# The V projection by seven block products for eight, over token halves, pairs of k tiles and column halves

## The reference

```python
x = x + (y * silu(gate)) @ a_w_out[layer]            # end of layer 0
kv = _rmsnorm(x, kv_norm) @ w_kv                     # (512, 2048) @ (2048, 4096)
k = kv[..., :D_ATTN].reshape(bsz, s, 16, 128)
v = kv[..., D_ATTN:].reshape(bsz, s, 16, 128)
```

## Time and profile before

| | |
|---|---|
| median of 3 runs | 1697.44 us (1697.07 to 1697.75) |
| the profiled execution, its own time | 1697.99 us |
| its span | 1696.3 us |
| PE busy | 1681.1 us (99%) |
| PE weight loads busy | 1407.6 us (83%) |
| DVE busy | 895.3 us (53%) |
| ACT busy | 778.8 us (46%) |
| POOL busy | 229.1 us (14%) |
| DMA, mean | 101 GB/s |

### The profile page before, as it was taken

The page is one execution under the profiler, slowest core; times in us unless marked ns, Lnnn a source line. Parts: engine busy times, 40 slices in busy tenths (PEclk is TensorE's granted clock), DMA queues, the critical chain, the costliest instruction groups (busy, mean ns, idle before and its releaser), DMA issues.

```text
span 1696.3 us, 23428 instructions
## 1 busy us (share of the span) xinstructions
PE 1681.1 (99%) x7839; PEld 1407.6 (83%) x7839; DVE 895.3 (53%) x1600; ACT 778.8 (46%) x1542; POOL 229.1 (14%) x219
## 2 busy tenths in 40 slices
PE   8999999999999999999999999999999999999998
PEld 6888888888888888888888888888888888888888
DVE  5666676666765343442223556464655556463333
ACT  7655566665555232333334544454444535432223
POOL 0121221112112010120000111111111111112100
PEclk9999999999999999999999999999999999999999
DMA  5333333333332222333343322223232232323223
GB/s 183 100 102 97 99 94 98 93 97 95 103 97 98 94 99 93 98 94 120 123 123 120 103 92 85 94 87 99 75 105 88 91 98 76 106 75 115 92 96 134
DMA packets 154269, 170.87 MB, mean 101 GB/s; under 512 B 9992, under 2 KB 135128, under 8 KB 154072
## 3 DMA queue, kind: packets, MB, share of 16 engines
q1 hardware_dynamic: 154200, 170.02, 31.8%
HBM read 161.59 MB, written 8.39 MB: 100 GB/s over the span
## 4 chain that ended last, share of the span: by engine, by line
PE 98%; ACT 1%; DVE 0%; DMA 0%; issue 0%; POOL 0%; SPq 0%; POOLq 0%; DVEq 0%; ACTq 0%
PE ps L398 96%; PE ps L537 1%; PE ps L427 0%; DMA xraw<-in_x 0%; PE ps L582 0%; DVE rbuf L1056 0%; POOL y_lo L1257 0%; ACT w_hi L641 0%; PE ps L434 0%; ACT abuf L729 0%; DVE w_lo L909 0%; DVE tbuf L1052 0%; ACT L729 0%; ACT rbuf L717 0%; ACT tbuf L726 0%
## 5 line engine op out<-in xcount | busy, mean ns | idle before, releaser
L398 PE MATMUL ps<-x_hi,w_hi 128*128 128x512 f32 x1408 | 551.5, 392 | 0.0
L398 PE MATMUL ps<-x_hi,w_lo 128*128 128x512 f32 x1408 | 548.7, 390 | 0.0
L398 PE MATMUL ps<-x_lo,w_hi 128*128 128x512 f32 x1408 | 548.6, 390 | 0.0
L917 DVE SCALAR_TENSOR_TENSOR w_lo<-stage,cT,w_hi 128x256 fp32r<-128x256 f32 x352 | 198.8, 565 | 393.0 <-ACT w_hi L649 384.1
L647 ACT ACTIVATE w_hi<-stage,cT 128x256 fp32r<-128x256 f32 x352 | 178.7, 508 | 375.6 <-PE ps L398 375.5
L398 PEld LDWEIGHTS ps<-x_hi,w_lo 128*128 128x128 f32 x1408 | 264.6, 188 | 55.3
L398 PEld LDWEIGHTS ps<-x_hi,w_hi 128*128 128x128 f32 x1408 | 264.8, 188 | 53.9 <-issue 0.4
L398 PEld LDWEIGHTS ps<-x_lo,w_hi 128*128 128x128 f32 x1408 | 264.7, 188 | 53.6 <-issue 0.2
L909 DVE TENSOR_TENSOR w_lo<-stage,w_hi 128x512 fp32r<-128x512 f32 x160 | 129.1, 808 | 241.6 <-ACT w_hi L641 241.6
L641 ACT ACTIVATE w_hi<-stage 128x512 fp32r<-128x512 f32 x160 | 100.6, 631 | 265.2 <-PE ps L398 264.0
L919 DVE SCALAR_TENSOR_TENSOR w_lo<-stage,cT,w_hi 128x256 fp32r<-128x256 f32 x352 | 180.5, 513 | 0.0
(11 more groups left out here) (164 smaller groups left out, 2035.0 us busy)
## 6 DMA issues: line engine op xcount, KB each, us to landing
stage<-in_a_w_in SPq DMA_DIRECT2D x160, 256.0 KB, 2.7
stage<-in_w_kv SPq DMA_DIRECT2D x128, 256.0 KB, 2.6
stage<-in_b_w_in SPq DMA_DIRECT2D x128, 256.0 KB, 2.6
stage<-in_a_w_out SPq DMA_DIRECT2D x80, 256.0 KB, 2.7
stage<-in_b_w_out SPq DMA_DIRECT2D x64, 256.0 KB, 2.5
v_scratch<-v_f SPq DMA_DIRECT2D x16, 256.0 KB, 3.9
v_lo<-v_scratch SPq DMA_DIRECT2D x8, 512.0 KB, 4.4
out<-x SPq DMA_DIRECT2D x8, 512.0 KB, 3.3
```

What stands on the lines that cost most here:

```text
L398: mm = pe.matmul(dst, a, b, start=start and n == 0, stop=stop and n == 2, skip_group_check=not check)
L917: nc.vector.scalar_tensor_tensor(w_lo[:, slot, 0:256], stage[:, slot, 0:256], cT[:, col:col + 1], f(w_hi[:, slot, 0:256]), ALU.mult, ALU.s ...
```

## The change

V is cut into blocks: tokens in halves (A1x, A2x), the k tiles in 8 pairs i of an even and an odd tile (Ax1, Ax2), the columns in two groups g of 1024, each in halves of 512. For each g and i the weights are the blocks b11, b12 (even tile), b21, b22 (odd tile), and seven products are made where four blocks of A by four of B would take eight:

- sums of the activations, once for all: S1 = A21 + A22, S2 = S1 - A11, S3 = A21 - A11 (as the code has it, by halves of `x1`), S4 = S2 less A12; they are made by POOL in stage 2 into `s_raw`, rounded by ACT into `s_hi`, the rest taken by DVE (S2 of i < 4) or POOL (all others) into `s_lo`;
- sums of the weights, for each g and i: t1 = b11 - b12 (POOL, `first_block`, once in sweep a and again in sweep b), b22g = gain * b22 (ACT, `block22`), t2 = gain * t1 + b22g, t3 = gain * b11 - t2, t4 = gain * b21 - t2 (all DVE, `block_sum`);
- each of the seven right-hand operands is then split by ACT (`operand_hi`) and DVE (`operand_lo`) into a ring of six pairs of buffers.

The products (operands) of a group are numbered q in three sweeps: a: p1, p6 for i = 0..7 (16), b: p7, p5 for i = 0..7 (16), y: p2, p4, p3 for i = 0..7 (24). Each takes 2 token tiles x 3 matmuls of 512 columns. There are 2 x 56 = 112 of them. At fixed places DVE joins the banks (u2, u3, c22, c21, c12, two instructions of 128 x 512 each) and ACT scales the results. Blocks are loaded by sweep, so b11 and b12 come twice and b22 twice: 112 loads of 256 KB where there were 64, in seven buffers. Stage 2 and the first 12 units of stage 3 are rewritten around this; the rest of the program stays.

The core of the diff:

```diff
+VG, VP = 2, KD // 2
+NO = 7 * VP
+VOPS = VG * NO
+VRING, AHEAD_V = 6, 5
...
+V_LOADS = [(g, sweep, i, block) for g in range(VG)
+           for sweep, blocks in (("a", ("b11", "b12", "b22")), ("b", ("b11", "b12")), ("y", ("b21", "b22")))
+           for i in range(VP) for block in blocks]
+V_SLOT = [0, 1, 2, 3, 1, 2, 0] + [(4, 5, 6, 3, 1, 2, 0)[n % 7] for n in range(len(V_LOADS) - 7)]
...
+            def block_read(n):
+                g, sweep, i, block = V_LOADS[n]
+                m = 2 * VP * g + (VP if sweep == "b" else 0) + i
+                if block == "b12" or block == "b11":
+                    sp.wait_ge(t1_ready, m + 1)
+                if sweep == "a" and block == "b11":
+                    sp.wait_ge(op_lo, OPERAND[g, i, "p1"] + 1)
...
-            def unit_v(c, j):
...
-                    mm = product(ps[4 * (c % 2) + t][:, :], x_hi[:, j, P * t:P * t + P], x_lo[:, j, P * t:P * t + P],
-                                 w_hi[:, s, :], w_lo[:, s, :], j == 0, j == KD - 1)
...
+            def value_product(q):
...
+                if name == "p4" and i == 0:
+                    pe.wait_ge(u3_ready, 2 * g + 2)
+                if name == "p3" and i == 0:
+                    pe.wait_ge(c22_ready, 2 * g + 2)
+                if name in V_SUM and g == 0:
+                    pe.wait_ge(s_lo_ready[V_SUM[name][0]], i + 1)
+                pe.wait_ge(op_lo, q + 1)
...
+                for t in range(2):
...
+                    mm = product(ps[banks[t]][:, :], left[0], left[1], hi_w, lo_w,
+                                 i == 0 and name in ("p1", "p6", "p7", "p5"), i == VP - 1, check=False)
+                mm.then_inc(op_used, 1)
...
+            def block22(q):
+                g, i, name = operand(q)
+                n = V_AT[g, "a", i, "b22"]
+                act.wait_ge(v_full[V_SLOT[n]], V_FULL[n])
+                if VP * g + i:
+                    act.wait_ge(t2_ready, VP * g + i)
+                nc.scalar.activation(b22g_at(g, i), v_block(g, "a", i, "b22"), ACT.Identity,
+                                     scale=kv_gain(2 * i + 1)).then_inc(b22g_ready, 1)
...
+            def value_step(q):
+                if q + 2 < VOPS and operand(q + 2)[2] == "p6":
+                    block22(q + 2)
+                if q >= 0:
+                    operand_hi(q)
...
+            def block_sum(q):
+                g, i, name = operand(q)
+                n = VP * g + i
+                if name == "p6":
+                    dve.wait_ge(t1_ready, 2 * VP * g + i + 1)
+                    dve.wait_ge(b22g_ready, n + 1)
+                    if g == 0 and i == 1:
+                        dve.wait_ge(w_used, U3)
+                    nc.vector.scalar_tensor_tensor(t2_at(g, i), t1[:, i % 2, :], kv_gain(2 * i), b22g_at(g, i),
+                                                   ALU.mult, ALU.add).then_inc(t2_ready, 1)
+                elif name == "p7":
+                    at = V_AT[g, "b", i, "b11"]
+                    dve.wait_ge(v_full[V_SLOT[at]], V_FULL[at])
+                    if n:
+                        dve.wait_ge(op_lo, OPERAND[(n - 1) // VP, (n - 1) % VP, "p7"] + 1)
+                    nc.vector.scalar_tensor_tensor(t3[:, :], v_block(g, "b", i, "b11"), kv_gain(2 * i), t2_at(g, i),
+                                                   ALU.mult, ALU.subtract).then_inc(t3_ready, 1)
...
+            def make_u3(g):
+                dve.wait_ge(op_used, OPERAND[g, VP - 1, "p7"] + 1)
+                if g:
+                    dve.wait_ge(v_stored, 16 * 8 * g)
+                for t in range(2):
+                    dve.wait_ge(u2_ready, 2 * g + t + 1)
+                    nc.vector.tensor_tensor(v_f[:, 2 + t, 512:1024], u2[:, t, :], ps[4 + t][:, :],
+                                            ALU.add).then_inc(u3_ready, 1)
...
+            def value_step(q):
+                if q + 1 < VOPS:
+                    block_sum(q + 1)
+                if q >= 0:
+                    operand_lo(q)
+                for i, step in S2_HI_AT.items():
+                    if step == q and i < 4:
+                        sum_lo(S2, i)
+                g, o = divmod(q, NO)
+                if o == 2 * VP + AHEAD_V:
+                    make_u2(g)
+                if o == 4 * VP + AHEAD_V - 1:
+                    make_u3(g)
+                if o == 4 * VP + AHEAD_V:
+                    make_c22(g)
...
+                if m >= 2:
+                    h, e = divmod(m - 2, 2 * VP)
+                    if e < VP:
+                        pool.wait_ge(t2_ready, VP * h + e + 1)
+                    else:
+                        pool.wait_ge(op_lo, OPERAND[h, e - VP, "p5"] + 1)
+                nc.gpsimd.tensor_tensor(t1[:, m % 2, :], v_block(g, sweep, i, "b11"), v_block(g, sweep, i, "b12"),
+                                        ALU.subtract).then_inc(t1_ready, 1)
...
+            for i in range(VP):
+                first_block(0, "a", i)
+                if i == 3:
+                    token_sums(VP - 1)
+                if i >= 4:
+                    sum_lo(S2, i)
+                    sum_lo(S3, i - 4)
+            for i in range(VP):
+                first_block(0, "b", i)
+                sum_lo(S1, i)
+                if i < 4:
+                    sum_lo(S3, i + 4)
+            sum_lo(S4, 0)
+            sum_lo(S4, 1)
+            squares(VP - 1)
+            for i in range(2, VP):
+                sum_lo(S4, i)
...
```

More of the change, by code:

```diff
@@ L145, in build @@
+        u2 = x1
         with ExitStack() as mem34:
@@ new lines, in block_load @@
+            def block_load(n):
+                slot = V_SLOT[n]
+                before = [e for e in range(n) if V_SLOT[e] == slot]
+                if before:
+                    block_read(before[-1])
+                elif slot < RING:
+                    sp.wait_ge(lo_ready, U3 - RING + slot + 1)
+                else:
+                    sp.wait_ge(w_used, U3)
+                g, sweep, i, block = V_LOADS[n]
+                row = P * (2 * i + (block in ("b21", "b22")))
+                col = D + 1024 * g + 512 * (block in ("b12", "b22"))
+                sp.dma_start(v_block(g, sweep, i, block), w_kv[row:row + P, col:col + 512]).then_inc(v_full[slot], 16)
@@ L350, in v_load @@
             def v_load(p):
                 sp.dma_start(f(v_lo[:, :, :]), v_scratch[:, :, at(p * (2 * P), 2 * P)]).then_inc(v_in, 16)
[L353 to L357 removed]
+            for n in range(len(V_LOADS)):
+                block_load(n)
+                if n == len(V_LOADS) // 2 + 3 * VP:
+                    v_store(0)
@@ L500, in _ @@
[L500 to L511 removed]
+            V_LEFT = {"p1": (x_hi, x_lo, 0, 0, (2, 3)), "p2": (x_hi, x_lo, 1, 0, (2, 3)),
+                      "p4": (x_hi, x_lo, 1, 256, (4, 5))}
@@ new lines, in token_sums @@
+            def token_sums():
+                pe.wait_ge(acc_step, 2 + KD)
+                pe.wait_ge(p6_taken, 2)
+                for t in range(TT):
+                    mm = pe.matmul(ps[0][:, t:t + 1], acc[:, P * t:P * t + P], ones[:, 0:1],
+                                   start=True, stop=True)
+                mm.then_inc(stat_ready, 1)
+            for q in range(VOPS):
+                if q == STAT_AT:
+                    token_sums()
+                if q == SPREAD_AT:
+                    spread(2, ps[1])
+                value_product(q)
@@ L764, in body2 @@
             def body2(it, last):
                 for q in range(N2):
-                    hi_at(2, N2, U2, it, last, q)
-                    work2(it, q + LOOK)
-                    if last and q + LOOK == 26:
-                        act.wait_ge(sqrt_in, 2)
-                        nc.scalar.activation(small[:, 1, :], small[:, 1, :], ACT.Sqrt).then_inc(sqrt_out, 1)
+                    if not last or q + AHEAD < N2:
+                        hi_at(2, N2, U2, it, last, q)
+                    if last and q in (2, 3):
+                        sum_hi(S2, q - 2)
@@ new lines, in sum_lo, with make_u2 @@
+            def sum_lo(which, i):
+                dve.wait_ge(s_hi_ready[which], i + 1)
+                nc.vector.tensor_tensor(s_lo[:, which, i, :], s_raw[:, which, i, :], f(s_high(which, i)),
+                                        ALU.subtract).then_inc(s_lo_ready[which], 1)
+            def make_u2(g):
+                for t in range(2):
+                    dve.wait_ge(p6_taken, 2 * g + t + 1)
+                    nc.vector.tensor_tensor(u2[:, t, :], u2[:, t, :], ps[2 + t][:, :],
+                                            ALU.add).then_inc(u2_ready, 1)
```

461 lines of the change are left out of this document (357 added, 104 removed).

## The result

The changed kernel takes **1725.2 us** (median of 4 runs, 1722.89 to 1726.34), the kernel before beside it 1697.26: **1.0164 times as long, interval 1.0146 to 1.0181**. It is slower by 28 us, where +4.2 was predicted with an upper end of 1714. The profiled execution of the changed kernel took 1722.89 us, the shortest of the four.

The account below looks back on a forecast made before the run. It took PE, busy 99% of the span, as the bound. Removed matmuls -21.8, waits +18.5, +4.0 and +3.5 us sum to +4.2 on the median of 1697.44: 1701.6 us, range 1686 to 1714.

Parts of the forecast that it names:

- group 0, sweeps a and b: First two sweeps of group 0: 62.0 us of feeding against 43.5 of PE, so PE waits 18.5 us.
- group 0, sweep y: Start of group 0's third sweep: p4(0) waits for u3 behind DVE's other work, taken as 4.0 us.
- group 1: Second column group: DVE's 47.4 us of work against 44.9 of PE, plus p1's load chain; 3.5 us, of 1 to 7.
- the 48 further loads: Extra block loads of the V stage: costed at nothing, as 193 GB/s, 289 in sweep a, stays under the 392 seen.
- u3's wait: Before p4(0) of group 0: DVE makes u3 behind operand 36's rest; 3.0 to 6.1 us, taken as 4.0.
- the first 3.0 us: Start of group 0: the third t1 waits for a block load with its issue and semaphore, 3.0 us.
- The removal: V projection on PE: 768 matmuls become 672, the 96 worth 21.8 us.
- The turns: V stage: POOL and DVE instructions reading two SBUF tiles alternate; 57.6 us in sweeps a and b of group 0.
- The 256-column form: POOL's 256-column instruction, not in the trace: holds DVE for 0.52 us, bounds 0.25 and 1.04.
- Rival 1: POOL slips into DVE's gaps; sweeps a and b of group 0 end near 53, 1689 us in all; chance 0.28.
- rival 2: POOL and DVE shut each other out for whole instructions: 9 us more in group 0, 3 in group 1, 1713.6; chance 0.10.
- Rival 3: PE's clock falls through waiting: group 0 at 1.2 GHz, +54 us, 1755 us; chance 0.04.

Follow-up runs that it names:

- sums_late: dve_order_hi with POOL's last two squares put behind operand 43 and its four sums of the last pair behind operand 8: 1700.35 us, ratio 1.0016.
- hi_first: The changed kernel with ACT issuing the first part of a sum ahead of the copy of the second next b22: 1719.34 us, ratio 1.0127.
- pool_order_hi: The changed kernel with joins and c11 earlier, stores later, ACT's first part ahead of the copy; POOL keeps its sums: 1706.5 us, ratio 1.0055.
- pool_short: The changed kernel with POOL's V-stage instructions cut short, most of its sums left out, waits and loads kept: 1697.0 us, ratio 0.9997.
- dve_order_hi: The changed kernel with t1 and S rests on DVE, joins and c11 earlier, stores later, ACT's first part ahead of the copy: 1697.59 us, ratio 1.0003.

## Why the prediction was wrong

It had the direction that it thought likeliest (slower, 0.46) and a size that was far off: +4.2 for +28. Against the sum, in us that PE lost:

| step of the prediction | forecast | measured | what was missed |
|---|---|---|---|
| group 0, sweeps a and b | 18.5 | 22.8 | +4.3 |
| group 0, sweep y | 4.0 | 10.2 | +6.2 |
| group 1 | 3.5 | 15.3 | +11.8 |

Three steps failed. The largest is group 1: the turns of DVE and POOL were summed there as if DVE were full, and the 48 further loads were costed at nothing (3.5 us for 15.3). Next is the start of sweep y, which had u3's wait and nothing behind it (4.0 for 10.2), then the assumption that the shared path is never idle behind the first 3.0 us (18.5 for 22.8). In all three the clock stood at nothing. These 48.3 us less 21.8 and the 1.6 below make the 24.9 us between the two profiled executions; the other 3 of the 28 lie between those two executions and the medians.

**The removal** was right: 672 matmuls, 154 us with the small ones, and no other stage paid: outside the V projection the two profiled executions differ by 1.6 us, in favour of the changed kernel.

**The turns** were right, in their price and their sum. Sweep b by the prediction's prices is 8 x (2 x 0.66 + 0.60 + 1.04 + 0.52) + 4 x 0.52 = 29.9 us; it was 29.41, and 29.4 in every version in which POOL does all of its work in full. (The sum leaves out u2, two instructions that read PSUM.) The 256-column form, bounded by 0.25 and 1.04 and taken as 0.52, shows in the changed kernel and, alone, in sums_late:

```profile
735.75 0.94 DVE L1424 TENSOR_TENSOR s_lo<-s_raw,s_hi 128x256 fp32r<-128x256 f32 x1
...
738.85 1.66 POOL L1707 TENSOR_TENSOR t<-stage 128x512 f32<-128x512 f32 x1 [0.43 <-issue]
739.29 1.77 DVE L1411 SCALAR_TENSOR_TENSOR w_lo<-v_stage,cT,w_hi 128x512 fp32r<-128x512 f32 x1
```

```profile
738.44 0.42 DVE L1425 TENSOR_TENSOR s_lo<-s_raw,s_hi 128x256 fp32r<-128x256 f32 x1
```

0.94 - 0.42 = 0.52, and 1.77 - 0.75 = 1.02 for the 512-column form. Rival 1 (turns overlap) would have had a and b end near 53, and rival 2 (whole instructions) sweep b at 29.9 + 8 x 0.25 + 12 x 0.23 = 34.7. Neither did. (The 66.4 us of a and b alone don't speak against rival 1, since they hold other losses too; sweep b and the 0.52 do.)

**Group 0, sweep a: the sum of turns was taken for the whole.** 62.0 less 29.9 leaves 32.1 for a; it took 37.0. I saw that the fourth operand's ACT step stands behind `block22` and its load, and then assumed all the same that the shared path is never idle behind the first 3.0 us. DVE's busy time is 30.65 of 36.98: 6.3 us idle, 3.4 of it in that very chain, and about 1.2 us were clock. hi_first takes 2.3 us out of this sweep.

**Group 0, sweep y: a mis-sized term and two that were not there.** u3 cost 4.9 us, inside my 3.0 to 6.1. The 12 matmuls behind it at 1.2 GHz cost 12 x 0.20 = 2.4, and c11, taken by ACT behind operand 59's first part, 2.2; the prediction has no line for either.

**Group 1 was forecast by the wrong model.** I summed DVE's and POOL's turns, as if DVE were full. In sweep a DVE was idle for 9 of 26.6 us. The prediction did name the chain from the rest of p1 through a load, t1 and t2 to the next rest, but gave it at most 1 us per two pairs, 4 in the group, and 3.5 for all of it. The waits of SP, ACT and DVE around that sweep:

```profile
SPq L464 <- DVE w_lo L1411: 13.2, 3, 5.2
ACT b22g L937 <- DMA v_stage<-in_w_kv: 5.5, 2, 3.8
DVE w_lo L1418 <- ACT w_hi L962: 3.6, 1, 3.6
DVE v_wlo L1418 <- ACT v_whi L962: 3.2, 1, 3.2
```

DVE waited for sums whose blocks were late, because SP got their buffers late; ahead of sweep b SP had the eight stores in front as well. "Costed at nothing" stood beside the 48 further loads: by bandwidth they do fit (212 GB/s in the fastest sweep), but a load is also a link from DVE's last read of a buffer to its next read. Without the loads the two sweeps fall from 55.2 to 46.3 us. Some 5 of the 15.3 us are clock, in three of the five stretches (about 24 matmuls x 0.20), and 1.8 are the second wait for u3.

**Rival 3, the clock,** was right in kind and wrong in form. I priced only a whole group at 1.2 GHz (+54, chance 0.04), from one row in which the clock reads 1.00 at the start of the program. It came in five stretches, 7.2 us in all. It also explains why order is worth more than its waits: in the profiled execution of pool_order_hi the clock is 1.00 in the whole stage, so some 7 of the 17.7 us between the two profiled executions are clock. *The Trainium skill (TensorE: Matmul & The Clock Gate, section HAM oscillation — how this bites in real kernels) describes the clock going down and up again inside a kernel; the windows above agree. The prediction took from that page only the loss after idling.*

**The causes overlap**, which is why the single cuts sum to more than 28 us. POOL's turns take the lead away that hides a late join, a late c11, a late copy and a late load. With no turns the old order costs nothing that the 96 matmuls don't pay (pool_short, 1697.0); with the sums on DVE it takes the new order too. What is shown is that both are enough for most of it, and that neither version has anything of the 21.8 us left. Where the last 12 us of sweep a of group 0 go is open in part: in dve_order_hi 8 of them are waits that DVE's rest terms ended, and 2.6 the clock (13 slow matmuls in one stretch of 6.8 us). DVE is busy 32.12 of the 33.99 us of that sweep and 25.27 of the 25.89 of the next, so with the sums on it DVE's own work fills both; what the turns of POOL's last squares and sums add to it isn't settled.

## What to carry to other kernels

Before taking matmuls away from a full PE, count the lead that the feeding engines have, not their busy share: here DVE went from a third of the stage to 83 and 96% of the first two sweeps, and every wait that lead had hidden (a join, a copy ahead of a sum, a store ahead of a load) came out at once. Price turns on a shared path by the stretch beside the other engine; that gave sweep b within 2%. Then walk each chain through buffers back to the load, and count with a long wait of PE the slow matmuls that may follow it. An instruction needed soon goes ahead of those needed later, in each queue, before anything is optimised for its own cost.

## What was not expected of the hardware

- POOL's fills ran beside DVE's two-input instructions at no cost to them: 0.74 us beside two fills, as alone, and 0.94 for half the columns beside a sum, where 0.42 is what they take alone.
- The clock came down in single stretches of 3.4 to 6.8 us and back, five times in the stage. In sweep b of group 0, where PE's waits are many and short, it stayed at 1.00.
- Eight stores of 256 KB in one go took SP 5.53 us here, 0.69 each, where four took 1.96 before, 0.49 each.
